# Norm, projection and attention layer: the first norm's 1/rms moved behind the input projection

## The reference, cut to what matters

```
h    = x * rsqrt(mean(x*x, axis=-1) + EPS) * ln1_g       # first norm
proj = h @ w_in                                          # 1024 -> 1976 columns
h_q, h_kv, h_kr, q_b, kv_b, gate_b = split(proj)         # 384, 256, 32, 512, 768, 24
o_a  = mla_mixer(h_q, h_kv, h_kr, ...)                   # rms_norm(h_q) @ w_uq, rms_norm(h_kv) @ w_ukv, attention
o_b  = nsa_mixer(q_b, kv_b, gate_b, ...)                 # three attention branches, mixed by sigmoid(gate_b)
x    = x + concat(rms_norm(o_a), rms_norm(o_b)) @ w_o
x    = x + square(relu(rms_norm(x) @ w_up)) @ w_down
```

## Time and profile before

| | us |
|---|---|
| median of 3 runs | 762.5 (761.69 to 763.08) |
| profiled execution, its own time | 762.94 |
| span of the profiled execution, first to last instruction | 760.8 |
| TensorE busy | 707.8 (93% of the span) |
| VectorE, ScalarE, GpSimd busy | 365.4, 292.3, 109.4 |

### The profile page before, as it was taken

One profiled execution on the slowest core, in us unless ns is written; L12 is line 12 of the kernel. 1 busy time (PEld: TensorE's weight loads), 2 busy tenths in 40 slices (PEclk: granted clock), 3 DMA queues, 4 the chain that ended last, 5 costly groups with the idle time before them and its releaser, 6 DMA issues.

```text
span 760.8 us, 10039 instructions
## 1 busy us (share of the span) xinstructions
PE 707.8 (93%) x3735; PEld 602.7 (79%) x3735; DVE 365.4 (48%) x704; ACT 292.3 (38%) x630; POOL 109.4 (14%) x160
## 2 busy tenths in 40 slices
PE   7987679999989979988879999999999999999998
PEld 5976457888878968877769888888888888888886
DVE  4645554646687654563665554522323545431311
ACT  5554444445667432253623433321111434321110
POOL 2424664210042210112410000000000000000000
PEclk9999899999999979997999999999999999999999
DMA  7430213102035100010003323232323232323302
GB/s 266 124 108 28 87 56 112 61 5 80 1 111 160 63 1 1 1 57 28 29 1 111 111 84 111 84 111 84 111 84 110 84 111 83 111 84 110 98 1 96
DMA packets 17953, 60.04 MB, mean 79 GB/s; under 512 B 2120, under 2 KB 2248, under 8 KB 17906
## 3 DMA queue, kind: packets, MB, share of 16 engines
q1 hardware_dynamic: 16562, 55.41, 21.9%
q0 software_dynamic: 1200, 3.94, 1.6%
q10 hardware_dynamic: 144, 0.07, 0.0%
HBM read 57.26 MB, written 2.15 MB: 78 GB/s over the span
## 4 chain that ended last, share of the span: by engine, by line
PE 83%; DVE 6%; ACT 3%; issue 3%; POOL 3%; DMA 1%; SPq 0%; DVEq 0%; ACTq 0%; POOLq 0%
PE bank L1391 14%; PE bank L1393 14%; PE bank L1392 14%; PE bank L1693 8%; PE bank L1695 8%; PE bank L1694 8%; PE bank L1412 6%; PE bank L1579 5%; PE bank L1539 2%; PE bank L1621 1%; PE bank L1546 1%; DVE w_lo L909 1%; DMA x<-x 1%; PE bank L1553 1%; ACT w_hi L601 1%
## 5 line engine op out<-in xcount | busy, mean ns | idle before, releaser
L909 DVE TENSOR_TENSOR w_lo<-raw,w_hi 128x1024 fp32r<-128x1024 f32 (+3 forms) x97 | 112.5, 1166 | 130.3 <-ACT w_hi L601 130.2
L601 ACT ACTIVATE w_hi<-raw 128x1024 fp32r<-128x1024 f32 (+3 forms) x97 | 97.3, 1009 | 119.6 <-PE bank L1393 118.2
L1693 PE MATMUL bank<-act_hi,w_hi 128*128 128x512 f32 (+3 forms) x288 | 106.8, 371 | 0.0
L1695 PE MATMUL bank<-act_hi,w_lo 128*128 128x512 f32 (+3 forms) x288 | 106.7, 370 | 0.0
L1694 PE MATMUL bank<-act_lo,w_hi 128*128 128x512 f32 (+3 forms) x288 | 106.7, 370 | 0.0
L1391 PE MATMUL bank<-w_hi,a_hi 128*128 128x512 f32 x256 | 99.6, 389 | 0.0
L1392 PE MATMUL bank<-w_lo,a_hi 128*128 128x512 f32 x256 | 99.6, 389 | 0.0
L1393 PE MATMUL bank<-w_hi,a_lo 128*128 128x512 f32 x256 | 99.6, 389 | 0.0
L1391 PE MATMUL bank<-w_hi,act_hi 128*128 128x512 f32 (+3 forms) x224 | 92.2, 412 | 2.6 <-DVE act_lo L922 2.6
L1392 PE MATMUL bank<-w_lo,act_hi 128*128 128x512 f32 (+3 forms) x224 | 81.2, 362 | 0.0
L1393 PE MATMUL bank<-w_hi,act_lo 128*128 128x512 f32 (+3 forms) x224 | 81.1, 362 | 0.0
(11 more groups left out here) (188 smaller groups left out, 1106.6 us busy)
## 6 DMA issues: line engine op xcount, KB each, us to landing
raw<-weights SPq DMA_DIRECT2D x86, 512.0 KB, 3.3
raw<-weights SPq DMA_DIRECT2D x7, 384.0 KB, 4.3
x<-x SPq DMA_DIRECT2D x4, 512.0 KB, 6.9
bias<-bias_by_distance POOLq DMA_DIRECT2D x1, 2048.0 KB, 9.2
y<-x SPq DMA_DIRECT2D x8, 256.0 KB, 2.2
raw<-weights SPq DMA_DIRECT2D x4, 288.0 KB, 2.8
raw<-weights SPq DMA_DIRECT2D x4, 280.0 KB, 2.9
consts<-consts SPq DMA_DIRECT2D x1, 688.0 KB, 4.3
```

Of the source, the lines that this page charges most:

```text
L601: act.activation(w_hi[:, m % RING, 0:width], raw[:, n % RAW, 0:width], ACT.Copy).then_inc(*hi_done.mark(n))
L909: dve.tensor_tensor(w_lo[:, m % RING, 0:width], raw[:, n % RAW, 0:width], w_hi[:, m % RING, 0:width].bitcast(F32), ALU.subtract).then_inc( ...
L1693: pe.matmul(dst, h[:, ws], act_hi[:, k, cols], start=k == 0, stop=False)
L1695: ins = pe.matmul(dst, l[:, ws], act_hi[:, k, cols], start=False, stop=k == KD - 1)
```

## The change

The row scaling of the first norm multiplies by the gain only and waits for x instead of for 1/rms. The four squares move in ScalarE's order from between the early splits and copies to behind split 4. All instructions that bring a block of the projection out of PSUM (cq, ckv, nq, nkv, cmp) take the tile's 1/rms as their scale, 52 instructions in all; the gates' exponential takes its negative, rs_neg, which GpSimd computes in one more instruction behind the fourth rsqrt. cq_out also waits for the tile's 1/rms, and the first instruction of row_in for cmp waits for rs_neg.

```
--- before.py
+++ after.py
@@ -332,6 +332,7 @@
             return stats[:, stat_at[0] - n:stat_at[0]]
 
         ss_ln, rs_ln = stat(NT), stat(NT)
+        rs_neg = stat(NT)
         ss_c, rs_c, ss_kr = stat(2 * NT), stat(2 * NT), stat(NT)
         ss_row, rs_row = stat(16), stat(16)
         neg_max = stat(8 * 2)
@@ -459,6 +460,8 @@
             for t in range(NT):
                 pool.wait_ge(*squares.at(("ln1", t)))
                 rsqrt(("ln1", t), rs_ln[:, t:t + 1], ss_ln[:, t:t + 1], D_MODEL)
+            pool.wait_ge(*rsqrt_done.at(("ln1", NT - 1)))
+            pool.tensor_scalar(rs_neg, rs_ln, -1.0, 1.0, ALU.mult, ALU.mult).then_inc(*pool_step.mark("neg"))
             pool.dma_start(onehot, a["onehot"]).then_inc(*onehot_in.mark("table"))
 
 
@@ -622,33 +625,34 @@
                 for half in range(2):
                     to_hi(("ln1", t, half), act_hi[:, 4 * half:4 * half + 4, t * P:(t + 1) * P], 4, P)
 
-            ln1_square(0)
             split_hi(SPLITS[0])
-            for t in range(1, NT):
+            for t in range(NT):
+                ln1_his(t)
+                if t < NT - 1:
+                    split_hi(SPLITS[t + 1])
+            split_hi(SPLITS[4])
+            for t in range(NT):
                 ln1_square(t)
-                ln1_his(t - 1)
-                split_hi(SPLITS[t])
-            ln1_his(NT - 1)
-            split_hi(SPLITS[4])
 
 
             def cq_out(t):
                 key = ("cq", t)
                 act.wait_ge(*dense_done.at(key))
+                act.wait_ge(*rsqrt_done.at(("ln1", t)))
                 if t:
                     act.wait_ge(*squares.at(("cq", t - 1)))
-                act.activation(square[:, 0:Q_RANK], cq_bank(t)[:, 0:Q_RANK], ACT.Square, accum_out=ss_c[:, t:t + 1]).then_inc(*squares.mark(key))
-                act.activation(c_row[:, t, 0:Q_RANK], cq_bank(t)[:, 0:Q_RANK], ACT.Copy).then_inc(*copied.mark(key))
+                act.activation(square[:, 0:Q_RANK], cq_bank(t)[:, 0:Q_RANK], ACT.Square, scale=rs_ln[:, t:t + 1], accum_out=ss_c[:, t:t + 1]).then_inc(*squares.mark(key))
+                act.activation(c_row[:, t, 0:Q_RANK], cq_bank(t)[:, 0:Q_RANK], ACT.Copy, scale=rs_ln[:, t:t + 1]).then_inc(*copied.mark(key))
 
             def ckv_out(t):
                 key = ("ckv", t)
                 bank = ckv_bank(t)
                 act.wait_ge(*dense_done.at(key))
                 act.wait_ge(*squares.at(("ckv", t - 1) if t else ("cq", NT - 1)))
-                act.activation(square[:, KV_RANK:KV_RANK + ROPE], bank[:, KV_RANK:KV_RANK + ROPE], ACT.Square, accum_out=ss_kr[:, t:t + 1]).then_inc(*squares.mark(("kr", t)))
-                act.activation(square[:, 0:KV_RANK], bank[:, 0:KV_RANK], ACT.Square, accum_out=ss_c[:, NT + t:NT + t + 1]).then_inc(*squares.mark(key))
-                act.activation(kr[:, t, :], bank[:, KV_RANK:KV_RANK + ROPE], ACT.Copy).then_inc(*copied.mark(("kr", t)))
-                act.activation(c_row[:, t, Q_RANK:], bank[:, 0:KV_RANK], ACT.Copy).then_inc(*copied.mark(key))
+                act.activation(square[:, KV_RANK:KV_RANK + ROPE], bank[:, KV_RANK:KV_RANK + ROPE], ACT.Square, scale=rs_ln[:, t:t + 1], accum_out=ss_kr[:, t:t + 1]).then_inc(*squares.mark(("kr", t)))
+                act.activation(square[:, 0:KV_RANK], bank[:, 0:KV_RANK], ACT.Square, scale=rs_ln[:, t:t + 1], accum_out=ss_c[:, NT + t:NT + t + 1]).then_inc(*squares.mark(key))
+                act.activation(kr[:, t, :], bank[:, KV_RANK:KV_RANK + ROPE], ACT.Copy, scale=rs_ln[:, t:t + 1]).then_inc(*copied.mark(("kr", t)))
+                act.activation(c_row[:, t, Q_RANK:], bank[:, 0:KV_RANK], ACT.Copy, scale=rs_ln[:, t:t + 1]).then_inc(*copied.mark(key))
 
             def latent_hi(name, t):
                 lo, n = (0, 3) if name == "cq" else (3, 2)
@@ -740,9 +744,10 @@
                 bank = D[bank_of("D", key)]
                 j = t % 2
                 if b == "cmp":
+                    act.wait_ge(*pool_step.at("neg"))
                     act.wait_ge(*scaled.at(("nkv", NT - 2 + t // 2)))
-                    act.activation(raw_cmp[:, t, :], bank[:, 0:256], ACT.Copy).then_inc(*copied.mark(("raw", t)))
-                    act.activation(gates[:, t, :], bank[:, 256:280], ACT.Exp, scale=-1.0).then_inc(*copied.mark(key))
+                    act.activation(raw_cmp[:, t, :], bank[:, 0:256], ACT.Copy, scale=rs_ln[:, t:t + 1]).then_inc(*copied.mark(("raw", t)))
+                    act.activation(gates[:, t, :], bank[:, 256:280], ACT.Exp, scale=rs_neg[:, t:t + 1]).then_inc(*copied.mark(key))
                     return
                 before = (b, t - 1) if t else ("nq", NT - 1) if b == "nkv" else None
                 if before:
@@ -751,14 +756,14 @@
                 if two:
                     act.wait_ge(*scaled.at(two))
                 if b == "nq":
-                    act.activation(square, bank, ACT.Square).then_inc(*squares.mark(key))
-                    act.activation(raw_row[:, j, :], bank, ACT.Copy).then_inc(*copied.mark(key))
+                    act.activation(square, bank, ACT.Square, scale=rs_ln[:, t:t + 1]).then_inc(*squares.mark(key))
+                    act.activation(raw_row[:, j, :], bank, ACT.Copy, scale=rs_ln[:, t:t + 1]).then_inc(*copied.mark(key))
                 else:
                     src = bank.rearrange("p (b v n) -> p b v n", b=2, v=2)
                     two_b = lambda r: r[:, 0:256].rearrange("p (b n) -> p b n", b=2)
-                    act.activation(two_b(square), src[:, :, 0, :], ACT.Square).then_inc(*squares.mark(key))
-                    act.activation(n_v[:, t, :, :], src[:, :, 1, :], ACT.Copy).then_inc(*copied.mark(("nv", t)))
-                    act.activation(two_b(raw_row[:, j, :]), src[:, :, 0, :], ACT.Copy).then_inc(*copied.mark(key))
+                    act.activation(two_b(square), src[:, :, 0, :], ACT.Square, scale=rs_ln[:, t:t + 1]).then_inc(*squares.mark(key))
+                    act.activation(n_v[:, t, :, :], src[:, :, 1, :], ACT.Copy, scale=rs_ln[:, t:t + 1]).then_inc(*copied.mark(("nv", t)))
+                    act.activation(two_b(raw_row[:, j, :]), src[:, :, 0, :], ACT.Copy, scale=rs_ln[:, t:t + 1]).then_inc(*copied.mark(key))
 
             def unit_step(n, last):
 
@@ -922,15 +927,14 @@
                 dve.tensor_tensor(dst, src, hi.bitcast(F32), ALU.subtract).then_inc(*turn_lo.mark(key))
 
             def ln1_rows(t):
-                dve.wait_ge(*rsqrt_done.at(("ln1", t)))
+                dve.wait_ge(*x_in[t].at())
                 for half in range(2):
                     cols = slice(512 * half, 512 * half + 512)
                     if t == 0:
                         dve.wait_ge(*turned.at(("gain", half)))
                     if t >= 2:
                         dve.wait_ge(*turned.at(("ln1", t - 2, half)))
-                    dve.scalar_tensor_tensor(ln_row[:, t % 2, cols], x[:, t, cols], rs_ln[:, t:t + 1], D[half],
-                                             ALU.mult, ALU.mult).then_inc(*scaled.mark(("ln1", t, half)))
+                    dve.tensor_tensor(ln_row[:, t % 2, cols], x[:, t, cols], D[half], ALU.mult).then_inc(*scaled.mark(("ln1", t, half)))
 
             def ln2_rows(t):
                 dve.wait_ge(*rsqrt_done.at(("ln2", t)))
```

15 lines of the change are left out of this document (8 added, 7 removed).

## The result

The changed kernel took 771.38 us (median of 6 runs, 766.88 to 777.15) against 762.79 of the kernel before on the same chip: ratio 1.0116 (95% interval 1.0084 to 1.0148), slower. The profiled execution took 767.71 us with a span of 765.5, where before it was 762.94 and 760.8. The forecast was 765.2 with an upper end of 767.4. The direction was right, the size was not. All ratios leave out two executions that lie far above the others of their kernel, 780.72 us of *again_b* and 773.82 us of *spread*; medians and means have them in.

The account below looks back on a forecast made before the run. TensorE was taken to bound the kernel, carrying 83% of the chain. Terms of -2.4 + 3.75 + 0.35 + 1.0 summed to +2.7 us on the median of 762.5, giving 765.2 us, range 762.6 to 767.4.

Parts of the forecast that it names:

- Part 1: At the start, row scaling no longer waits for square and rsqrt: first projection at 9.2 instead of 11.32, 2.4 us gained.
- S: Point in ScalarE's order behind the fifth weight split where the four squares now begin, put at 24.85 us.
- Part 2: Squares build a queue on GpSimd ahead of cq's rsqrt; second ckv piece at S + 13.15, net 1.35 us later with Part 1.
- the queue is hidden: Rival: GpSimd's queue between last square and cq's rsqrt is short enough, so the start's gain remains: 760.4 us, chance 0.06.
- Part 3: Scale operand read from memory in 52 ScalarE instructions, only ckv_out(0)'s four on the path: 0.35 us (0 to 0.5).
- Part 4: TensorE's clock: new gaps before the second ckv piece may bring time at 1.2 GHz, 1.0 us lost (0 to 1.7).
- the start: Sign at the kernel's beginning: the first projection starts near 9.2 us.
- the squares: Sign on ScalarE: the squares run from about 25 us on.
- the tables ahead of cq's rsqrt: Sign on GpSimd: cq's first rsqrt comes near 35.5 us with the rotary tables directly ahead of it.
- the longer copies: Sign on ScalarE: copies with a scale take 0.1 us longer.
- Everything after 60 us shifted alike: Sign for the rest of the kernel: later stages only move by the same shift and keep their lengths.

Follow-up runs that it names:

- again_b: The changed kernel run again with no edit, against the kernel before: median 771.36 us, ratio 1.0089.
- spread: The changed kernel with its four squares placed in ScalarE's idle times behind splits 1, 2 and 3: 762.55 us, 1.0004 times the kernel before.
- again: The changed kernel run once more with no edit, beside the kernel before on one chip: median 767.5 us, ratio 1.0075.
- tables_first: The changed kernel with GpSimd's onehot load and rotary tables ahead of the first norm's rsqrt: 764.79 us, 1.0050 times the kernel before.
- operand: The kernel before with only the scale of the 52 instructions read from memory, a column of ones (minus ones for the gates): 763.07 us, ratio 1.0017.
- no_operand: The changed kernel without the 52 scale operands, squares and GpSimd's work kept: 766.70 us, 1.0065 times the kernel before.
- look_after_1: A further profile of the changed kernel with no edit, to see where its time at 1.2 GHz stands: span 766.2 us.
- spread_early: The spread kernel with weight splits 10 and 11 ahead of the copy of cq 3's transpose: 760.36 us, 0.9988 times the kernel before; repeated, 760.16 and 0.9974.

## Why the prediction was wrong

- **Part 1 held.** S was put at 24.85 and the first projection at 9.2; *again* shows 24.93 and 9.23, and 2.31 us won at the first ckv piece against 2.4. In the first profile the weights landed 0.5 later (split at 6.32) and 1.66 were left. Two more profiles of the kernel before start the first projection at 11.00 and 10.94 and the second ckv piece at 36.76 and 36.34, so all these differences are good to about 0.4.
- **Part 2 held, with 0.4 too little.** Second ckv piece at S + 13.55, forecast S + 13.15; rsqrt behind the tables at 35.70 in the first profile, forecast "near 35.5"; VectorE's split last, as forecast. Net 1.83 later in *again*, forecast 1.35. What was wrong here is a rival: "the queue is hidden" was priced at 760.4, as if only GpSimd's chain held TensorE. *tables_first* hides that chain, and ScalarE's stall of 2.07 us stays: 1.0050 times the kernel before, slower and not faster.
- **Part 3 held where it was named.** One operand costs 87 ns (taken: 0.12 us), and the wait at ckv grew by 0.36 (taken: 0.35), in *operand* and in the changed kernel. Whether the operands cost more elsewhere is open: at 40 us the runs give 0.9 (*operand*) and 1.3 (*no_operand*), each with a standard error of 0.5, and the traces of *no_operand* and *look_after_1* give 0.1 by the end. From 52.81 to 95.94 *again* loses 0.5 us more against the first profile of the kernel before, but only 0.1 and 0.3 against the other two.
- **Part 4 is the step that failed: the clock term, 1.0 us with a bound of 1.7.** It is 11.6 us more at 1.2 GHz (51.7 against 40.1), times 0.355, which is 4.1 us, with an error of about 0.8; in the first six runs it was 15.1 us more, which is 5.4. The forecast priced one stretch behind one gap, from the row at 50.62, as if it came about every second time. The runs show instead that four of five profiles have 3.3 or 6.9 us at 1.2 GHz ahead of 45 us, behind stalls of 1.72 us at most, and that more comes further on in part of the executions.
- **Sum.** 3.4 us at equal time at 1.2 GHz (forecast 1.7 for parts 1 to 3; 2.4 and 3.2 in the paired profiles) and 4.1 from the clock make 7.5, the difference of the means (770.0 and 762.5). Over all 21 runs the changed kernel's median is 768.4, also above the range's end of 767.4; that the first six came out at 771.38 is the clock's scatter. The sign of the forecast, slower, came out by its own mechanism, the queue that the squares build behind the start.

Of the signs named in advance, the start, the squares, the tables ahead of cq's rsqrt, 3.34 us of stalls between 32 and 39 (3.7 forecast) and the longer copies came as said. "Everything after 60 us shifted alike" holds in *again* to between 0.1 and 0.5 us, by the profile of the kernel before that it is held against.

**Open.** What makes the clock fall more often in the changed kernel is not shown. A mere shift (38.4 us), the late squares alone (40.9), the operand alone (41.3) and the queue alone (42.9) are not clear of the kernel before's 40.1. The four kernels above 45 us all have the new start, but *tables_first* (45.5, standard error 2.3), *spread* (47.7, 3.4) and *no_operand* (48.1, 3.4) are themselves only some two standard errors above 40.1, and the two *spread_early* runs have the new start too and stay at 39. So the new start as a cause of its own, without any stall, is neither shown nor excluded. Nor is it shown why *again* and *tables_first* went through the same stalls as the others without an early fall.

## What to carry to other kernels

When work is moved out of a start that is waited for, look at where it lands on each engine it passes through, and at every engine's own stall there, also those that seem covered by a longer one: taking away the longer one leaves the covered one. In the changed kernel ScalarE has idle times of 3.2, 3.1 and 4.3 us between 9.4 and 24.0 us; the same squares placed there, done by 21.3, added no stall on TensorE. And where TensorE has idle time early on, price the granted clock by repeated runs before trusting a forecast of a few tenths of a per cent: here it was worth as much as all of the moved work. The best gain (0.4%, about half of it by the clock) came from moving two ready splits ahead of a copy that waits.

## What the runs showed of the hardware beyond that

- The time at 1.2 GHz differs from run to run of one and the same kernel and explains most of its spread: 0.35 us of device time for each of its microseconds, in both kernels. A stretch at 1.2 GHz can begin behind stalls of 0.34 and 1.72 us (*look_after_1*), and the same stalls can pass without one (*tables_first*). The changed kernel's runs go from 765.49 to 780.72, those of the kernel before from 760.22 to 766.73.
- A squared row with a sum, 1024 columns, takes 1.06 us, and the next one that waits for its signal starts 1.24 behind it (25.58 to 26.82).
- GpSimd's power on one column took 0.55 us undisturbed, and beside splits on VectorE 0.94 (38.45 in the profile after) and 1.29. Its table products took 0.34 each where VectorE was idle and 0.58 where it was not.
